# Sample readout of a RetNet and HGRN2 layer: unsplit fp32 states through quarters of 32 array columns

## The reference, cut to what matters

```python
# retention: S_ret (128 x 256) per sample and head
S = gamma_h * S + k v^T
o_r = q S                      # 1 x 256
# HGRN2: S_hg (128 x 128) per sample and head
S = diag(f) S + (1 - f) i^T
o_h = S^T q                    # 1 x 128
# then: head RMSNorm of o_r and o_h, swish gates, output projections
```

## Time and profile before

| what | value |
|---|---|
| median of 3 runs | 1856.31 us |
| the profiled execution's own time | 1854.89 us |
| its span | 1853.1 us |
| mean granted TensorE clock | 0.995 |
| TensorE matmul busy | 1809.0 us, 98%, 14672 records |
| VectorE busy | 1148.3 us, 62% |
| ScalarE busy | 777.4 us, 42% |
| GpSimd busy | 278.5 us, 15% |

### The profile page before, as it was taken

How to read it: one execution, slowest core, us unless ns; L and a number is a source line. 1 busy time by engine, 2 the same in 40 slices (tenths; PEclk the granted TensorE clock), 3 DMA queues, 4 the chain that set the end, 5 groups by cost and what they waited for, 6 DMA issues and landing times.

```text
span 1853.1 us, 37457 instructions
## 1 busy us (share of the span) xinstructions
PE 1809.0 (98%) x14672; PEld 1789.6 (97%) x14672; DVE 1148.3 (62%) x1293; ACT 777.4 (42%) x894; POOL 278.5 (15%) x332
## 2 busy tenths in 40 slices
PE   5999999999999999999999999999999999999997
PEld 5999999999999999999999999999999999999996
DVE  8776877768777674555556665555555555545444
ACT  5444444444544453333334344443344334333332
POOL 4441624516235110000000000000000000000001
PEclk9999999999999999999999999999999999999998
DMA  7665646656467555555557655555655555555552
GB/s 230 191 203 171 195 139 194 203 174 195 139 191 209 174 165 178 180 181 177 175 168 229 187 177 181 177 176 178 181 177 176 179 180 176 182 181 179 175 180 102
DMA packets 387002, 333.86 MB, mean 180 GB/s; under 512 B 10240, under 2 KB 385024, under 8 KB 386816
## 3 DMA queue, kind: packets, MB, share of 16 engines
q1 hardware_dynamic: 368000, 318.87, 56.5%
q10 hardware_dynamic: 18944, 14.16, 2.6%
HBM read 316.67 MB, written 16.32 MB: 180 GB/s over the span
## 4 chain that ended last, share of the span: by engine, by line
PE 84%; DVE 6%; issue 3%; DMA 3%; ACT 1%; SPq 1%; POOL 0%; DVEq 0%; ACTq 0%
PE pA L1062 13%; PE pA L1063 13%; PE pA L1064 12%; PE pB L1063 11%; PE pB L1062 11%; PE pB L1064 11%; DMA raw<-in_w_in 3%; PE p L1062 3%; PE p L1063 3%; PE p L1064 3%; DVE lo L703 2%; PE p L1205 1%; DVE hg_scores L914 1%; PE p L1177 1%; SPq L358 1%
## 5 line engine op out<-in xcount | busy, mean ns | idle before, releaser
L703 DVE TENSOR_TENSOR lo<-raw,hi 128x1024 fp32r<-128x1024 f32 x568 | 724.2, 1280 | 575.7 <-ACT hi L407 569.7
L407 ACT CAST hi<-raw 128x1024 fp32r<-128x1024 f32 x568 | 595.6, 1049 | 847.8 <-PE pA L1064 355.9
L1062 PE MATMUL pA<-h_hi,hi 128*128 128x264 f32 x1728 | 500.4, 290 | 19.0 <-DVE lo L703 19.0
L1063 PE MATMUL pA<-h_lo,hi 128*128 128x264 f32 x1728 | 493.9, 286 | 0.0
L1064 PE MATMUL pA<-h_hi,lo 128*128 128x264 f32 x1728 | 493.4, 286 | 0.0
L1062 PE MATMUL pB<-h_hi,hi 128*128 128x264 f32 x1472 | 422.2, 287 | 0.0
L1063 PE MATMUL pB<-h_lo,hi 128*128 128x264 f32 x1472 | 418.8, 285 | 0.0
L1064 PE MATMUL pB<-h_hi,lo 128*128 128x264 f32 x1472 | 418.4, 284 | 0.0
L1062 PEld LDWEIGHTS pA<-h_hi,hi 128*128 128x128 f32 x1728 | 328.1, 190 | 22.7 <-issue 19.2
L1063 PEld LDWEIGHTS pA<-h_lo,hi 128*128 128x128 f32 x1728 | 327.5, 190 | 0.3
L1064 PEld LDWEIGHTS pA<-h_hi,lo 128*128 128x128 f32 x1728 | 327.3, 189 | 0.0
(11 more groups left out here) (250 smaller groups left out, 2486.2 us busy)
## 6 DMA issues: line engine op xcount, KB each, us to landing
raw<-in_w_in SPq DMA_DIRECT2D x224, 512.0 KB, 3.7
raw<-in_w_fin SPq DMA_DIRECT2D x176, 512.0 KB, 3.7
raw<-in_w_fout SPq DMA_DIRECT2D x88, 512.0 KB, 3.5
raw<-in_w_ret SPq DMA_DIRECT2D x32, 512.0 KB, 3.8
raw<-in_w_out SPq DMA_DIRECT2D x32, 512.0 KB, 4.1
S_ret<-in_s_ret SPq DMA_DIRECT2D x8, 1024.0 KB, 8.4
out_ret_s<-S_ret ACTq DMA_DIRECT2D x8, 1024.0 KB, 7.0
raw<-in_w_hg SPq DMA_DIRECT2D x16, 512.0 KB, 3.6
```

The lines of the kernel that those rows point to most:

```text
L407: copy(hi[s][:], raw[s][:]).then_inc(hi_done, 1)
L703: tt(lo[s][:], raw[s][:], hi[s][:].bitcast(F32), ALU.subtract).then_inc(split_done, 1)
L1062: mm(outs[t], w_hi, a_hi[:, kt, :], start=(kt == 0), stop=False)
L1063: mm(outs[t], w_hi, a_lo[:, kt, :], start=False, stop=False)
```

## The change

The queries are no longer split. Two fp32 buffers of 2 x 129 columns are cleared once at the start by GpSimd. Each head then copies the 8 query values into every 32nd column of them (`place_queries`), so that a block of 32 columns holds one sample's query in its column r and zeros elsewhere. The states are no longer split either. The readout becomes 16 fp32 products with 32 stationary columns, sample b = 4r + g in array columns 32g to 32g + 31, accumulated over r in PSUM rows 32g to 32g + 31. ScalarE copies all 128 PSUM rows (`o_rows`) before it issues the state stores. Three full 128 x 128 transposes follow in `tail`, and VectorE picks two rows of every quarter by a copy. The state stores wait for the state updates in place of the state splits. The constants lose 64 columns, and the counts of parts_done and masked change with what is left.

```diff
+        q_only = alloc(heads, "q_only", [P, 2, NS * 16 + 1])
+        hq_only = alloc(heads, "hq_only", [P, 2, NS * 16 + 1])
-        q_parts = alloc(heads, "q_parts", [P, NS, 2], F32R)
-        hq_parts = alloc(heads, "hq_parts", [P, NS, 2], F32R)
-        q_only = alloc(heads, "q_only", [P, NS, 2, NS], F32R)
-        hq_only = alloc(heads, "hq_only", [P, NS, 2, NS], F32R)
-        o16 = alloc(heads, "o16", [2 * NS, 384])
+        o_rows = alloc(heads, "o_rows", [P, 384])
-        S_ret_hi = alloc(heads, "S_ret_hi", [P, NS, RV], F32R)
...
@@ scalar, i == 15, 16, 18
-                        act.wait_ge(p56_free, h * N56 + (OUT1 + 2))
-                        copy(S_ret_hi[:, 0:4, :], S_ret[:, 0:4, :]).then_inc(state_hi, 1)
-                        act.wait_ge(p56_free, h * N56 + (OUT1 + 3))
-                        copy(S_ret_hi[:, 4:8, :], S_ret[:, 4:8, :]).then_inc(state_hi, 1)
-                        act.wait_ge(p56_free, h * N56 + (OUTH4 + 2))
-                        copy(S_hg_hi[:], S_hg[:]).then_inc(state_hi, 1)
@@ scalar, i == 19
-                        act.wait_ge(state_split, h * 3 + 3)
+                        act.wait_ge(p7_full, h * N7 + (RD3 + 1))
+                        copy(o_rows[:], p7[:, 0, 0:384]).then_inc(p7_free, 1)
+                        act.wait_ge(p56_free, h * N56 + (OUTH4 + 2))
                         act.dma_start(hg_s[...], S_hg[:]).then_inc(state_out, 16)
                         act.dma_start(ret_s[...], S_ret[:]).then_inc(state_out, 16)
-                        act.wait_ge(p7_full, h * N7 + (RD3 + 1))
-                        copy(o16[:], p7[0:2 * NS, 0, 0:384]).then_inc(p7_free, 1)
@@ gpsimd, start
+            nc.gpsimd.memset(q_only[:], 0.0).then_inc(query_rows_clear, 1)
+            nc.gpsimd.memset(hq_only[:], 0.0).then_inc(query_rows_clear, 1)
@@ vector
+            def place_queries(out, q):
+                return nc.vector.tensor_copy(
+                    out[:, :, 0:128].rearrange("p r (g j) -> p r g j", g=4)[:, :, :, 0],
+                    q.rearrange("p (r g) -> p r g", r=2)).then_inc(queries_placed, 1)
@@ vector, tail i == 0
-                    nc.vector.tensor_reduce(oT[:, :, NP:T], by_part[:, 0:2], AX.X, ALU.add).then_inc(sample_outputs, 1)
-                    nc.vector.tensor_reduce(ohT[:, NP:T], by_part[:, 2], AX.X, ALU.add).then_inc(sample_outputs, 1)
+                    of_sample = p4[:, 0, 0:384].rearrange("p (e g r) -> p e r g", e=3, g=4)[:, :, 0:2]
+                    nc.vector.tensor_copy(oT[:, :, NP:T].rearrange("p e (r g) -> p e r g", r=2), of_sample[:, 0:2]
+                                          ).then_inc(sample_outputs, 1)
+                    nc.vector.tensor_copy(ohT[:, NP:T].rearrange("p (r g) -> p r g", r=2), of_sample[:, 2]
+                                          ).then_inc(sample_outputs, 1)
@@ vector, i == 3 (i == 7 the same for q)
-                        query_parts(hq_parts, hquery[:, NP:T], h, 1)
-                        dve.wait_ge(parts_done, h * 14 + 4)
-                        masked_query(hq_only[:], hq_parts[:])
+                        if first:
+                            dve.wait_ge(query_rows_clear, 2)
+                        place_queries(hq_only, hquery[:, NP:T])
@@ vector, i == 15, 17, 18
-                            state_lo(S_ret_lo[:, 0:4, :], S_ret[:, 0:4, :], S_ret_hi[:, 0:4, :], h, 0)
-                        state_lo(S_ret_lo[:, 4:8, :], S_ret[:, 4:8, :], S_ret_hi[:, 4:8, :], h, 1)
-                        state_lo(S_hg_lo[:], S_hg[:], S_hg_hi[:], h, 2)
@@ tensor, tail i == 0
-                    one16 = c_ident[0:2 * NS, 0:2 * NS]
-                    mm(p4[:, 0, 0:16], o16[:, 0:128], one16, start=True, stop=True)
-                    for e in range(1, 3):
-                        last = transpose(p4[:, 0, 16 * e:16 * e + 16], o16[:, e * 128:e * 128 + 128], one16)
+                    for e in range(3):
+                        last = transpose(p4[:, 0, e * P:e * P + P], o_rows[:, e * P:e * P + P], c_ident)
@@ tensor, i == 19
-                    pe.wait_ge(state_split, h * 3 + 2)
-                    for query, states, cols in ((q_only, (S_ret_hi, S_ret_lo), slice(0, RV)),
-                                                (hq_only, (S_hg_hi, S_hg_lo), slice(RV, 384))):
-                        if query is hq_only:
-                            pe.wait_ge(state_split, h * 3 + 3)
-                        for b in range(NS):
-                            for n, part in enumerate(states):
-                                last = mm(p7[0:2 * NS, 0, cols], query[:, b].rearrange("p c j -> p (c j)"),
-                                          part[:, b, :], start=(b == 0 and n == 0), stop=(b == NS - 1 and n == 1))
+                    pe.wait_ge(queries_placed, h * 2 + 2)
+                    pe.wait_ge(p56_free, h * N56 + (OUTH4 + 2))
+                    for query, state, cols in ((q_only, S_ret, slice(0, RV)), (hq_only, S_hg, slice(RV, 384))):
+                        rows = query[:].rearrange("p r x -> p (r x)")
+                        for r in range(2):
+                            for g in range(4):
+                                b = 4 * r + g
+                                last = mm(p7[32 * g:32 * g + 32, 0, cols], rows[:, 32 * b:32 * b + 32], state[:, b, :],
+                                          start=(r == 0), stop=(r == 1), tile_position=(0, 32 * g))
```

More of the change, by code:

```diff
@@ L89 @@
 K_GAMMA = K_KDEC + 2 * H
-K_EYE8 = K_GAMMA + H
-K_ROW8 = K_EYE8 + NS * NS
+K_ROW8 = K_GAMMA + H
 K_SIZE = K_ROW8 + NS
@@ L278, in build @@
         rg_sig_done = sem("rg_sig_done")
-        state_hi = sem("state_hi")
-        state_split = sem("state_split")
+        query_rows_clear, queries_placed = sem("query_rows_clear"), sem("queries_placed")
         sample_outputs = sem("sample_outputs")
@@ L785, in level_psum @@
                 return bass.AP(tensor=p56, offset=64 * n, ap=[[2 * 512, P], [512 + 64, 2], [1, 64]])
-            def state_lo(out, state, state_hi_part, h, n):
-                dve.wait_ge(state_hi, h * 3 + (n + 1))
-                tt(out, state, state_hi_part.bitcast(F32), ALU.subtract).then_inc(state_split, 1)
             def tail(i, h):
@@ L859, in head @@
                         dve.wait_ge(rotated, h * 3 + 3)
[L860 to L863, removed]
+                        key_parts(k_parts, qk[:, 1, NP:T], h, 1)
+                        place_queries(q_only, qk[:, 0, NP:T])
                     elif i == 11:
@@ L867, in head @@
                         for e in range(2):
-                            value_parts(v_parts[:, e], vT[:, e, NP:T], h, 4 + e)
+                            value_parts(v_parts[:, e], vT[:, e, NP:T], h, 2 + e)
                         dve.wait_ge(keys_copied, h + 1)
                         masked_keys(k_only[:], p7[0:8 * NS, 0, 256:384])
-                        dve.wait_ge(masked, h * 3 + 3)
+                        dve.wait_ge(masked, h + 1)
                         dve.sem_inc(p7_free, 1)
@@ L1090, in sample_updates @@
             def sample_updates(q, h):
-                pe.wait_ge(masked, h * 3 + 3)
+                pe.wait_ge(masked, h + 1)
                 for b in range(4):
@@ L1121, in attend @@
                     pe.wait_ge(p7_free, h * N7 + (TK0 + 1))
-                    pe.wait_ge(parts_done, h * 14 + 6)
+                    pe.wait_ge(parts_done, h * 10 + 4)
                     natural(p7[:, 0, 0:256], qk[:, 1, :], 128)
@@ L1132, in attend @@
                     pe.wait_ge(p56_free, h * N56 + (TV0 + 1))
-                    pe.wait_ge(parts_done, h * 14 + 12)
+                    pe.wait_ge(parts_done, h * 10 + 8)
                     for e in range(2):
@@ L1161, in attend @@
                     pe.wait_ge(p7_free, h * N7 + (TI2 + 1))
-                    pe.wait_ge(parts_done, h * 14 + 14)
+                    pe.wait_ge(parts_done, h * 10 + 10)
                     natural(p7[:, 0, 0:256], hig[:, 0, :], 128)
```

10 lines of the change are left out of this document (2 added, 8 removed).

## The result

The median of 4 runs is 1836.49 us (1835.52 to 1837.11), beside 1856.38 us for the kernel before in 4 runs: a ratio of 0.9891, 95% interval 0.9874 to 0.9908. That is 19.9 us less, where 5.5 less was forecast and the range ended at 1839. The profiled execution took 1836.31 us; its span is 1834.5, 18.6 less than before.

A forecast was written before the change was run, and what follows sets the result against it. It took TensorE's stream of matmuls, plus places where TensorE stands still, as the bound. Readout +1.6, tail's transposes -2.6 and wait for the value parts -4.5 sum to -5.5 us: median 1856.31 to 1850.8, range 1839 to 1863.

The forecast's parts named there:

- The readout: TensorE's readout per head: two passes in flight, products starting in program order; 3.09 us against 2.89, +1.6 us over 8 heads.
- the rival of full overlap: Readout: passes of all four quarters run at once; 1.68 us a head, 1839.5 us in all; chance 0.22.
- The edges: Readout: going in and out of quarters on TensorE, taken at 0.19 us twice, 0.38 a head.
- The rival that it made, 1868: Readout: quarters run in sequence because stationary loads wait for products in flight; 5.58 us a head, 1868 in all; chance 0.13.
- The tail's transposes: Tail of each head: three full transposes at 0.33 us replace three tiny operations at 0.65; -2.6 us in all.
- The wait for the value parts: Transposes at i = 13, six heads: less VectorE work brings the late weight chunk sooner, 0.75 of 1.18 us; -4.5 us.
- Costed at nothing: ScalarE's three state copies and VectorE's three subtractions a head run beside TensorE's projection products, so removing them counts zero.
- each pass pays its load: Readout: passes overlap by two, but 16 stationary loads a head lie open; +12.4 us, 1863 in all; chance 0.10.
- the wait doesn't move: Transposes at i = 13: the chunk is late for the states ahead, not VectorE; -1.0 us in all, 1855; chance 0.10.

The follow-up runs named there:

- one quarter: Changed kernel with all 16 readout products placed in the first column quarter, accumulated over all eight samples: 1868.36 us.
- six passes in a row: Changed kernel with the readout written quarter by quarter for three products (six passes), then each quarter's second S_hg product: 1848.42 us.
- the grouped order: Changed kernel with the readout's two loops swapped, so that the two products of a quarter stand next to each other: 1836.74 us.
- two quarters: Changed kernel with the readout's products over two column quarters instead of four, accumulated over four samples each: 1845.33 us.
- a whole quarter at a time: Changed kernel with the quarter as the outermost readout loop, so four products (eight passes) of one quarter stand in a row: 1857.08 us.

## Why the prediction was wrong

**The readout** is the step that failed: "Two passes are in flight, not eight and not four." Four are. It rested on "I take it that products start in program order, as every timeline here shows them". Those timelines show products that use the whole array, or one place in it, and say nothing of two quarters. The same row was then held against the rival of full overlap, where it has no more weight. The passes' prices (0.215 and 0.11) were right, and so was the rival's sum: 1.30 + 0.38 = 1.68, measured 1.64. The edges, taken at twice 0.19, measure 0.11 going in and 0.22 coming out (the last S_hg product starts at 613.92, and 0.11 later the next could start; it does at 614.25).

The rule of the Trainium skill, "TensorE: Matmul & The Clock Gate", section on packing small matmuls, that a set of tiles costs one product's time and about 4 ns for each further tile, agrees with this case: three passes start within 0.02 us, and the readout takes 1.64. The rival of full overlap was given 0.22. The rule of the same page of the Trainium skill that a stationary load overlaps products in flight only where the row group differs does not hold across quarters: eight loads that all use 128 rows lie within 0.16 us while passes run. The rival that it made, 1868, is what one quarter alone takes (1868.36), for another reason: there the passes themselves stand in one queue.

**The tail's transposes**: -2.6 forecast, -2.5 by the rows; right.

**The wait for the value parts**: its cause was right, as far as putting the query work back brings the wait back in seven heads. How many heads wait depends on more than that, though: with VectorE's query work as in the kernel after, it is five heads with one quarter (2.9 us in TensorE's waits) and with six passes in a row, and one with the grouped order, two quarters and a whole quarter at a time. What sets this was not found. The size was short, -5.6 for -4.5. One reason is seen: the next instruction starts 0.32 us behind the copy, where 0.6 had been taken from the length of a cast's record. What counts on VectorE is the step to the next start, as it had been for TensorE.

**What was left out**: the same VectorE work also held TensorE's own next chunk, a wait of 0.2 us in the view of waits, in six heads. The prediction asked only for the longest wait behind the masking and not for the short one. That is -1.7 us, and the wait comes back with the query work.

**Costed at nothing**: it held as an accounting of the kernel before, since nothing of the gain needs these splits. It would not have held for a kernel that kept them, and the cover that the prediction named, the projection products, was not the only one: the old readout was another, under which VectorE's `rg_gate` had 1.25 us more. The removal is worth 3 to 4 us, but only once the readout is short. So the terms here do not simply add.

**The rest**: the rivals *each pass pays its load* and *the wait doesn't move* did not occur. The forecast said that it would be wrong if the readout fell outside 2.7 to 3.8 us, and it did. With the readout at 1.64 and the other terms as they stood, its sum is 1839.2, all but the rival's 1839.5. The remaining 2.7 us are the two waits.

## What to carry to other kernels

Small products placed in different column quarters run together, so order them so that no quarter has more than four passes (two full fp32 products) in a row. With eight in a row the readout took 4.30 us, which gives back 2.66 of the 3.88 us between one quarter (5.52) and four (1.64). A row in which two products use the same place in the array says nothing of products that don't. When a stretch of TensorE is shortened, look for what the other engines did under it, and when VectorE work ahead of the loads is removed, count the short waits as well as the long one.

## What the runs showed of the hardware

- Quarters take their passes independently and out of program order: four passes start within 0.1 us, eight stationary loads within 0.16.
- A quarter holds four passes, the running one among them, and a pass for a full quarter stops all that is behind it. Shown by steps of 0.89 us with eight passes in a row and 0.46 with six. Whether the limit counts passes, their loads, whole products of two passes or something behind them was not separated.
- Going into products placed in 32 columns and out again costs 0.32 to 0.38 us together, in the first quarter too. Transposes with 32 stationary columns that name no place don't pay it. That is in line with the page "TensorEngine Tiling (Array Packing)" of the Trainium skill, Key Properties, by which a change of tiling mode drains TensorE.
- Not shown: rounded halves in quarters, one pass each. By the steps of the earlier trace rows, 32 such products over four quarters would take an estimated 16 x 0.117 / 4 + 16 x 0.060 / 4 = 0.71 us in place of 1.30. No run places them so.
